# Layer 0's expert rows sent through DRAM as layer 1's are, and the second round's choice made one pair ahead

## What is computed

```python
    g_idx = jnp.argmax(g_prob, axis=-1)
    e_logits = jnp.take_along_axis(e_logits, g_idx[:, None, None], axis=1)[:, 0]
    top_v, top_i = lax.top_k(e_logits, TOP_K_IN_GROUP)
    e_w = jax.nn.softmax(top_v, axis=-1) * g_w
    expert = g_idx[:, None] * EXPERTS_PER_GROUP + top_i
    gate = jnp.sum(jax.nn.one_hot(expert, N_EXPERTS, dtype=jnp.float32) * e_w[..., None], axis=1)
    hg = jnp.einsum('td,edf->tef', t, w1)
    hu = jnp.einsum('td,edf->tef', t, w3)
    a = jax.nn.silu(hg) * hu * gate[..., None].astype(t.dtype)
    y = jnp.einsum('tef,efd->td', a, w2)
```

## Time and profile before

| what | us |
|---|---|
| median of three runs | 829.5 (826.95 to 829.72) |
| the profiled execution, in all | 825.66 |
| its span, first to last instruction | 823.9 |
| TensorE busy | 761.6 (92%) |
| VectorE, ScalarE, GpSimd busy | 230.6, 163.8, 50.3 |
| moved by DMA | 289.64 MB, mean 352 GB/s |
| a pair of layer 0, of layer 1's first three | 27.30, 23.70 |

### The profile page before, as it was taken

How to read it: one execution, slowest core, us unless ns; L and a number is a source line. 1 busy time by engine, 2 the same in 40 slices (tenths; PEclk the granted TensorE clock), 3 DMA queues, 4 the chain that set the end, 5 groups by cost and what they waited for, 6 DMA issues and landing times.

```text
span 823.9 us, 10497 instructions
## 1 busy us (share of the span) xinstructions
PE 761.6 (92%) x4071; PEld 428.3 (52%) x4071; DVE 230.6 (28%) x653; ACT 163.8 (20%) x372; POOL 50.3 (6%) x74
## 2 busy tenths in 40 slices
PE   4899879999999999999799999999996989999796
PEld 4487458754344434443488758673333353333344
DVE  2301331531111111011779931442121112111115
ACT  2210230430100010001503852441100000110012
POOL 5032000000000000000100000001000000001000
PEclk9899999979999999999999999979998999999988
DMA  9997999779999999999995359578999709999941
GB/s 300 399 398 279 412 408 431 309 282 423 424 429 426 426 428 426 426 427 413 397 398 222 129 224 426 190 279 355 429 424 421 340 15 414 431 424 425 424 176 54
DMA packets 42639, 289.64 MB, mean 352 GB/s; under 512 B 4417, under 2 KB 5901, under 8 KB 30290
## 3 DMA queue, kind: packets, MB, share of 16 engines
q1 hardware_dynamic: 36752, 275.78, 81.7%
q0 software_dynamic: 5056, 11.98, 3.9%
q10 hardware_dynamic: 770, 1.06, 0.4%
HBM read 285.63 MB, written 8.52 MB: 357 GB/s over the span
## 4 chain that ended last, share of the span: by engine, by line
PE 74%; DMA 13%; DVE 4%; issue 3%; ACT 2%; POOL 1%; SPq 1%; PEld 0%; DVEq 0%; PEldq 0%; POOLq 0%
PE ps L515 72%; DMA ring<-in_conv_w 4%; DMA back<-in_moe_w 4%; DMA ring<-in_w_in_ab 3%; DMA spare<-in_moe_w 3%; DVE work L1730 1%; PE ps L931 1%; SPq L461 1%; PE ps L799 1%; PE ps L733 1%; DVE rstd L1472 0%; ACT work L1160 0%; PE ps L770 0%; POOL work L1353 0%; ACT work L1156 0%
## 5 line engine op out<-in xcount | busy, mean ns | idle before, releaser
L515 PE MATMUL ps<-ring,work 128*64 128x512 f32 x1088 | 304.5, 595 | 2.7 <-issue 1.6
L515 PEld LDWEIGHTS ps<-ring,work 128*64 128x64 f32 x1088 | 94.6, 137 | 144.7 <-issue 144.4
L515 PE MATMUL ps<-back,ring 128*128 128x256 f32 x656 | 147.2, 385 | 7.8 <-DMA ring<-in_conv_w 2.6
L515 PEld LDWEIGHTS ps<-back,ring 128*128 128x128 f32 x656 | 124.0, 192 | 30.6 <-issue 4.2
L515 PE MATMUL ps<-bench,work 128*64 128x512 f32 x208 | 95.9, 609 | 1.6 <-DVE work L1688 1.4
L515 PE MATMUL ps<-spare,work 128*64 128x512 f32 x176 | 80.2, 610 | 4.8 <-issue 4.8
L515 PE MATMUL ps<-back,work 128*64 128x512 f32 x160 | 72.0, 597 | 0.0
L1730 DVE TENSOR_TENSOR work<-work,ps 128x256 f32<-128x256 f32 x34 | 19.4, 612 | 167.0 <-PE ps L515 167.0
L1897 DVE SCALAR_TENSOR_TENSOR work<-work,dw 128x256 f32<-128x256 f32 x120 | 50.9, 483 | 1.0
L1186 ACT ACTIVATE work<-ps 128x512 f32<-128x512 f32 x17 | 10.1, 597 | 199.8 <-PE ps L515 199.8
L515 PE MATMUL ps<-ring,csil 128*32 128x512 f32 x352 | 42.8, 623 | 1.7 <-DMA ring<-in_w_ada 1.7
(11 more groups left out here) (235 smaller groups left out, 627.2 us busy)
## 6 DMA issues: line engine op xcount, KB each, us to landing
ring<-in_moe_w SPq DMA_DIRECT2D x63, 2048.0 KB, 19.4
ring<-in_w_ada SPq DMA_DIRECT2D x22, 2048.0 KB, 19.1
bench<-in_moe_w SPq DMA_DIRECT2D x12, 2048.0 KB, 21.5
spare<-in_moe_w SPq DMA_DIRECT2D x11, 2048.0 KB, 20.2
back<-in_moe_w SPq DMA_DIRECT2D x10, 2048.0 KB, 21.7
ring<-in_conv_w SPq DMA_DIRECT2D x6, 2048.0 KB, 24.3
ring<-in_w_in_ab SPq DMA_DIRECT2D x2, 2048.0 KB, 25.2
ring<-in_w_out_ab SPq DMA_DIRECT2D x2, 2048.0 KB, 17.2
```

The costliest lines, as they stand in the source:

```text
L515: return nc.tensor.matmul(out, lhsT, rhs, start=start, stop=stop, skip_group_check=True)
```

## The change

Layer 0 is handled as layer 1: its first six pairs send their rows. The row buffers become two (`yrows[0]`, `yrows[1]`), as do the held places (`LAST_FREE`, `back_rows`). `place_tiles` hands pair 6's second w3 tile of layer 0 back only when pair 7's first w2 tile has been used, so that six loads after the stage each take the next place. GpSimd zeroes layer 0's buffer right after its pooling, from `mean4` instead of a corner of `work`, and layer 1's where the only one was. Second, `pick_more` is a buffer of its own for the second round's choice, which VectorE makes for every pair one pair ahead (`choose_more`); the second round then neither makes a choice nor remakes the first one. The core of the diff:

```diff
+            if STREAM[nxt] == ("w2", 0, 2 * PAIRS - 2) and slots[TILE[LAST_FREE[0]]] < BENCH:
+                free.append((slots[TILE[LAST_FREE[0]]], nxt))
+            if STREAM[nxt] == LAST_FREE[0]:
+                pass
+            elif slots[nxt] < BENCH or any(k[0] in ("w1", "w3", "w2") and k[1] == STREAM[nxt][1] for k in STREAM[n:]):
                 free.append((slots[nxt], nxt))
...
         def is_sent(l, i, r):
-            return l == 1 and r == 0 and i < SENT
+            return r == 0 and i < SENT
...
-                elif r == 0 and l == 1:
-                    add_sent(0)
+                elif r == 0:
+                    add_sent(l, 0)
...
-                    if l == 1 and 2 <= i:
-                        send_rows(i - 2)
+                    if 2 <= i:
+                        send_rows(l, i - 2)
+            def rows_back(l):
+                used(pool, LAST_FREE[l])
+                pool.wait_ge(y_sent, 16 * SENT * (l + 1))
+                for g in range(2):
+                    for c in range(2):
+                        a = c * NT + g * TG
+                        pool.dma_start(back_rows[l][:, c, g, :], yrows[l][a:a + TG, :]).then_inc(y_back[g], 16)
+            nc.gpsimd.memset(zero, 0.0).then_inc(zero_ready, 1)
+            pool.wait_ge(zero_ready, 1)
+            clear_rows(0)
+            pool.wait_ge(s_zero[0], 16)
             fetch_rows(0)
-            pool.wait_ge(round_done[0], PAIRS)
+            rows_back(0)
+            pool.wait_ge(round_done[0], PAIRS - SENT)
...
+            def choose_more(l, i):
+                shape = [P, 2, 2, CAP]
+                V.tensor_tensor(pick_more.rearrange("p g (u j) -> p g u j", u=2),
+                                iota[:, CAP:2 * CAP].unsqueeze(1).unsqueeze(1).to_broadcast(shape),
+                                slot[:, :, 2 * i:2 * i + 2].unsqueeze(3).to_broadcast(shape),
+                                ALU.is_equal).then_inc(more_ready, 1)
...
                 elif i + 1 < PAIRS:
                     choose_gate(i + 1, pick_ready[0])
+                    choose_more(l, i + 1)
...
-                        choose(l, i, 1, (picked[1], n + 1), pick_ready[1])
+                        dve.wait_ge(more_ready, n + 1)
+                        choose_gate(i, pick_ready[1], pick_more)
```

More of the change, by code:

```diff
@@ L116 @@
 SPARE, BENCH, BACK = SLOTS, SLOTS + 1, SLOTS + 2
+LAST_FREE = [("w3", l, 2 * SENT + 1) for l in range(2)]
 def place_tiles():
@@ L361, in backbone @@
         zero_ready = sem("zero_ready")
-        s_zero = sem("s_zero")
+        s_zero = [sem(f"s_zero{l}") for l in range(2)]
         y_sent = sem("y_sent")
@@ L391, in backbone @@
         dense_act_ready = sem("dense_act_ready")
-        picked = [sem(f"picked_round{r}") for r in range(2)]
+        picked = [sem("picked_round0")]
         gated = sem("gated")
-        picked_back = sem("picked_back")
+        more_ready = sem("more_ready")
         rest_ready = sem("rest_ready")
@@ L433, in backbone, with sent_before @@
         LAST_IN = ("in", 0, 2)
[L435 to L436 removed]
+        back_rows = [place(TILE[key]).rearrange("p (c g d) -> p c g d", c=2, g=2) for key in LAST_FREE]
         def is_sent(l, i, r):
[L440 removed]
+            return r == 0 and i < SENT
+        def sent_before(l, i):
+            return l * SENT + min(i, SENT)
         def ysel_count(l, i, r):
             n = i + l * PAIRS
[L445 removed]
+            return 2 * n - (sent_before(l, i) if r == 0 else 0)
         pe_at, act_at, dve_at = {}, {}, {}
@@ L807, in compact @@
                     turn_rows(1)
-                elif r == 0 and l == 1:
-                    add_sent(1)
+                elif r == 0:
+                    add_sent(l, 1)
                 tile_landed(l, i, 4)
@@ L1430, in _ @@
             last.then_inc(pads_ready, 1)
[L1431 to L1436, removed]
-            fetch_rows(1)
[L1438 to L1443, removed]
+            clear_rows(1)
+            pool.wait_ge(s_zero[1], 16)
+            fetch_rows(1)
+            rows_back(1)
         @block.vector
@@ L1632, in route @@
                 choose_pick(l, 1, 0, (picked[0], l * PAIRS + 2))
[L1634 to L1639, removed]
+                link(V.tensor_tensor(target.rearrange("p g (a e) -> p g a e", a=4), sel,
+                                 rg[:, 9].unsqueeze(2).to_broadcast([P, 2, 4, 4]), ALU.mult))
+                link(V.scalar_tensor_tensor(out=target, in0=target, scalar=float(NT), in1=wide(token_row, NE),
+                                        op0=ALU.mult, op1=ALU.add))
                 dve.wait_ge(gexp_out, 2 * l + 2)
@@ L1654, in route @@
                 take_at(l, 1, ps[:, 7, NT:NT + 1])
+                choose_more(l, 0)
             def take_at(l, i, found):
@@ L2005 @@
     args.append([nc.dram_tensor(f"hbuf{l}", (NT, D), F32, kind="Internal").ap() for l in range(2)])
-    args.append(nc.dram_tensor("yrows", (ROWS, D), F32, kind="Internal").ap())
+    args.append([nc.dram_tensor(f"yrows{l}", (ROWS, D), F32, kind="Internal").ap() for l in range(2)])
     for name, shape in OUTPUTS:
```

69 lines of the change are left out of this document (32 added, 37 removed).

## The result

The changed kernel takes 837.42 us (median of ten runs, 832.11 to 843.03), beside 828.87 us for the kernel before (826.92 to 830.56): a ratio of 1.0116, 95% interval 1.0088 to 1.0143. It is slower, by 8.6 us of medians; 835.2 us and +5.7 us were predicted, within a range of 828.0 to 843.5. So the side and the size are right, and the sum is 2.9 us short. The profiled execution of the changed kernel is one of the longer ones, 841.12 us in all, a span of 839.2.

A forecast was written before the change was run, and what follows sets the result against it. The DMA weight stream, not TensorE, was taken to bound layer 0's expert stage. Layer 0 +8.8, zeroing +0.9 and second round -4.0 gave +5.7 us on 829.5, so 835.2 us, range 828.0 to 843.5.

The forecast's parts named there:

- six sends: Layer 0, pairs 0 to 5: sending 1.40 MB of rows adds 3.6 us to the stream (3.3 to 8.0).
- rows read back: Layer 0, before the last tile: reading 2.10 MB of rows back adds 5.2 us to the stream (4.9 at full rate).
- last tile in all: End of layer 0's expert stage: sends and reads back together move the last tile by +8.8 us (8.2 to 13.2).
- TensorE's saving: Layer 0: TensorE has 18.2 us less to do, but none reaches the path, as it waits for tiles.
- layer 0 in all: Layer 0: the stream's added cost, with no further TensorE lag counted, makes +8.8 us.
- zeroing ahead: After layer 0's pooling: GpSimd's early filling of the row buffer partly exceeds the engines' idle time, +0.9 us (0.4 to 2.4).
- second round: Layer 1, pair 3: with the choice ready, TensorE starts at its own branch's end, -4.0 us (to -6.3).
- the stream is slower than TensorE in both layers: Expert stages: a pair's tiles need 29.5 us of DMA, against 27.30 (layer 0) and 23.70 us (layer 1) on TensorE.
- rows ride free: Layer 0, rival: weights keep 418 GB/s while rows pass, leaving only the second round's gain, about 824.5 us; chance 0.09.
- TensorE's lag: Behind layer 0's last tile: up to 4.9 us, the first 2.58 hidden, so 0 to 2.3 more; taken as 0.
- the -6.3: Layer 1, second round: the gain if the shorter stop also leaves the gather's clock at 2.4, 2.3 us more.
- Rival (d): Layer 0, pairs: waits for tiles lower TensorE's clock to 1.2 GHz; 843.2 us if the last two are late; chance 0.07.

The follow-up runs named there:

- no bytes in the sends: Changed kernel with every layer 0 row number outside the buffer, so its six sends skip all rows: 831.38 us, ratio 1.0038.
- nearly none read back: Changed kernel with each of layer 0's four reads back fetching 8 of its 128 rows: 829.16 us, ratio 1.0034.
- both together: Changed kernel, layer 0's sends skipping all rows, its reads fetching 8 of 128, its zeroing begun at about 140 us: 826.54 us, ratio 0.9980.
- the choice alone: Kernel before with only the second round's choice made one pair ahead, layer 0 unchanged: 823.54 us, ratio 0.9958; in a second series 824.62 us, 0.9963.

## Why the prediction was right, and where it was short

Term by term:

| term | predicted us | measured us | by |
|---|---|---|---|
| six sends | +3.6 (3.3 to 8.0) | +3.8; at the last tile +4.0 | no bytes in the sends |
| rows read back | +5.2 (4.9 to 5.2) | +5.6; at the last tile +4.0 | nearly none read back |
| last tile in all | +8.8 (8.2 to 13.2) | +9.6 | its landing |
| TensorE's saving | 0 | 0 | both together |
| layer 0 in all | +8.8 | +8.7 to +9.2 in four profiles, +10.2 in the fifth | stretches |
| zeroing ahead | +0.9 (0.4 to 2.4) | +3.3 (0.3 to 4.4) | early, with and without |
| second round | -4.0 (to -6.3) | -3.6; in the whole time -3.4 and -3.0 | layer 1, eleven profiles against two; the choice alone |
| sum | +5.7 | +8.4 | medians: +8.6 and +8.1 |

Layer 0 is counted from the one profile before (253.89 us). Two profiles of the choice alone, with the same layer 0, took 253.29 and 255.54, so the entry is good to about 1 us. Putting off the early zeroing was not clearly worth anything in the whole time (1.2 us, interval with zero); its 3.3 us are of the stretch alone.

**The stream.** The step from shares to "the stream is slower than TensorE in both layers" is what made the forecast, and the runs confirm each link: total rate unchanged, weights displaced, TensorE waiting. The sends, priced by queue 0's own share of the engines and not by the loss in a mixed stretch, came out within 0.4 us. The agreement for the reading back is in part luck: 5.2 was a price of the stream, and of the 5.6 us at the stage's end 2.2 are TensorE's clock; 2.4 us at the last tile stay when both sets of bytes are gone. Two rows were read loosely: the 25.13 us of the earlier trace rows are a piece of the chain, while that tile took 28.2 us from issue to landing, and the 0.15 us of the earlier trace rows are TensorE's idle time, 0.09 of it behind the landing. Neither changes the sum. The rule of the Trainium skill that was weighed there (DMA: Bandwidth & Descriptors, Issuing engines are not separate DMA queues) is borne out: the total was 425 GB/s with GpSimd's transfers and 426 without, and the forecast that rows ride free has nothing left.

**TensorE's lag** was put at 0 to 4.9 us behind the last tile, the first 2.58 hidden. It is 2.68 us. The last tile comes 9.6 us later, counted from the 33rd load; TensorE starts the convolution 12.2 us later (231.9 against 219.8), and the stage ends 8.7 later, because the convolution's first 32 records are done 3.5 us sooner after their start (the wait of 2.58 us is gone, and they lose 0.9 us less besides). One sentence on this was wrong: that the convolution's first wait would move by the same amount. It went away, because the zeroing for layer 1 moved too and the convolution's tile came only 5.6 us later (232.6 against 227.0 us from the 33rd load), ahead of TensorE. So part of the agreement of 8.8 with 8.7 is luck: the stream cost 0.8 us more than the forecast, and the convolution gave back 0.9 that the forecast didn't count.

**The zeroing** is the term that was mis-sized. Its step weighed the bytes against the idle share of one stretch of the stream and found 4.8 us of room for 5.2. On the stream that was fair: the tile behind it landed 2.1 us later, inside the bounds. What the step left out is what follows a longer wait on TensorE: the low clock behind it. Of the 3.3 us, 2.1 are the tile (1.5 in the wait for it, the rest ahead of that: four of the five show a wait of 0.4 to 0.5 us for the tile before) and 1.1 the next 40 records (6.7 us on the mean of the five against 5.6 without). Nothing is left for later: from the end of these records to the 33rd load it takes 72.8 us in the mean with the early zeroing and 72.7 without.

**The second round.** TensorE's stop fell from 7.35 to 3.61 us, and 3.5 was forecast. Its own branch is what is late next, as the step said: in the earlier trace rows it was through at 626.4, 3.3 us after the products ahead of it; now at

```profile
L901 PEldq COMPARE_BRANCH  x2: 75/1788/3501, 644.9 to 676.2; - x2
...
644.99 0.57 PE L526 MATMUL ps<-work,xtok 128*128 128x128 f32 x1 [3.61 <-issue]
```

and TensorE starts 0.1 us later. The gather behind it still runs at the low level (the stretch 644.9 to 651.5 us has a clock of 0.55) and took 6.58 us, where it had taken 6.11. So the -6.3 falls, and 0.5 of the 4.0 is lost.

**Rival (d),** the low clock in layer 0, happened in part. Behind the stops of 3.4 to 4.0 us in pairs 4 to 6, 16 records took 5.1 to 5.4 us instead of 3.65, and behind 4.74 us 32 records took 8.55; behind stops of 0.5 to 1.4 us nothing slowed. The stretch 284 to 308 us has a clock of 0.93, not 0.5. It costs only where the last pair is late. The Trainium skill's section on this (TensorE: Matmul & The Clock Gate, HAM oscillation) has an example with a wait at every step, each of them longer than the 2 to 3 us that were forecast here. The long stops in this trace agree with it and the short ones lie outside it, so the section didn't make this case the likely one, as the prediction read it; the measurement decides, and it was rightly not the forecast.

## What to carry to other kernels

Where two resources are full, cut the stage at the last tile and ask which of them already waits there; a change that buys one with bytes of the other is then decided by sign alone, and its price is a little more than bytes over the total rate (4.0 us for the 1.40 MB sent, where 426 GB/s gives 3.3). A filling or clearing transfer is often due late, so look for where the stream idles before placing it: moving one gained 2.2 us here, and the rows in layer 0 gained nothing. Price a longer wait with the clock behind it, not only with its length. And when bytes are taken out to price them, read the landing of the tile too: the end of the stage has the clock in it.

## What the runs showed of the hardware beyond that

The first 54 us, which the change doesn't touch, took 54.05 to 58.06 us in 13 profiled executions, and the three quoted above follow the granted clock between 30 and 45 us. That is nearly half of the effect under study: one profile beside another gave +15.5 us in all, the medians +8.6. Stretches between requests of the same load are the better ruler: layer 0 and layer 1 repeated to 0.1 us in the changed kernel. They aren't exact either: in the choice alone layer 0 differed by 2.3 us, with a wait and the clock behind it, and layer 1 ran from 236.0 to 239.5 us over the eleven profiles that have the new choice.

The same wait of 3.17 us for the same tile was followed by the low clock (1.2 GHz) in four executions, for some of the records at least, and by the full one (2.4) in a fifth. Behind a stop of 3.70 us in the kernel with neither set of bytes the granted clock was 1.00, and behind one of 1.81 us in the convolution of the choice alone it was 0.69:

```profile
304.40:311.40 7.00, 7.00 (x34) 2.80 (x36) 1.72 (x7) 0.00 (x0) 0.00 (x0) 1.00 1.02 426
```

```profile
414.30:419.80 5.50, 5.46 (x19) 4.54 (x19) 0.75 (x3) 0.01 (x1) 0.00 (x0) 0.69 1.05 391
```

So the length of a stop alone doesn't say what follows; here I have no rows that tell more.
